# Second block: attention jobs between eighths of the projection tiles, maps combined in one operation, head outputs written over the queries

## The reference, cut to what matters

```python
for l in range(2):                       # last = (l == 1)
    h, hc = modulate(rms(x)), modulate(rms(ctx))
    u, q, k, v = split_heads(h @ w_in);  uc, qc, kc, vc = split_heads(hc @ w_in)
    q, k = rope(q), rope(k)
    # diff_attn, per head: a0, a1 = softmax of two half-heads' scores
    #   o = (a0 - lam * a1) @ v     over all 768 keys (context and latent)
    mix = concat([pool_mixer(u), rms_head(o) * g_sub * (1 - lam_init)])
    x = x + ga * (mix @ w_out);  x = x + gm * mlp(x)
    if not last: the same for ctx, with its own 256 keys
```

## Time and profile before

| | us |
|---|---|
| median of 3 runs (lowest to highest) | 3059.66 (3058.81 to 3061.07) |
| the profiled execution | 3054.51 |
| its span in the profile | 3052.7 |
| layer 0: input stage, from 1411.09 | 176.2 |
| layer 0: attention, from 1587.31 | 152.6 |
| layer 1: input stage, from 2372.36 | 137.2 |
| layer 1: attention, from 2509.59 | 117.8 |

### The profile page before, as it was taken

How to read it: one execution, slowest core, us unless ns; L and a number is a source line. 1 busy time by engine, 2 the same in 40 slices (tenths; PEclk the granted TensorE clock), 3 DMA queues, 4 the chain that set the end, 5 groups by cost and what they waited for, 6 DMA issues and landing times.

```text
span 3052.7 us, 48183 instructions
## 1 busy us (share of the span) xinstructions
PE 2763.0 (91%) x20880; PEld 2199.7 (72%) x20880; DVE 1473.0 (48%) x2538; ACT 883.8 (29%) x1436; POOL 102.1 (3%) x168
## 2 busy tenths in 40 slices
PE   3999988888899999997968799999999888899998
PEld 1767566677788788886845478888888665678886
DVE  2455556678743544444256454333333546454344
ACT  2434411110133322233214433122232314333222
POOL 0000011112100000000010000000000000000000
PEclk7999999999999999998978799999999988999999
DMA  6000456630033222222010012111211120122320
GB/s 243 28 28 29 168 192 223 221 107 3 4 124 124 78 95 87 106 83 80 28 55 1 4 52 81 58 56 56 83 56 56 39 77 7 55 83 83 111 83 28
DMA packets 17922, 242.42 MB, mean 79 GB/s; under 512 B 2016, under 2 KB 2176, under 8 KB 2864
## 3 DMA queue, kind: packets, MB, share of 16 engines
q1 hardware_dynamic: 16416, 231.94, 20.8%
q0 software_dynamic: 1296, 7.39, 0.6%
HBM read 237.23 MB, written 2.10 MB: 78 GB/s over the span
## 4 chain that ended last, share of the span: by engine, by line
PE 84%; DVE 10%; ACT 3%; issue 2%; DMA 1%; POOL 0%; DVEq 0%; ACTq 0%; POOLq 0%
PE ps L317 58%; PE ps L1205 7%; PE ps L1912 2%; PE ps L379 2%; PE ps L1763 2%; PE ps L1933 2%; PE ps L859 1%; PE ps L815 1%; DVE hh L470 1%; DMA cst<-in_consts 1%; PE ps L861 1%; PE ps L860 1%; DVE mvec L2030 1%; PE ps L390 1%; DVE sq L466 1%
## 5 line engine op out<-in xcount | busy, mean ns | idle before, releaser
L317 PE MATMUL ps<-hh,ws 128*128 128x512 f32 x3936 | 943.0, 399 | 48.7 <-DVE hh L470 26.8
L317 PEld LDWEIGHTS ps<-hh,ws 128*128 128x128 f32 x3936 | 745.8, 191 | 228.6 <-issue 61.7
L308 DVE TENSOR_TENSOR ws<-raw,ws 128x1024 fp32r<-128x1024 f32 x295 | 360.0, 1223 | 220.5 <-ACT ws L300 220.4
L300 ACT ACTIVATE ws<-raw 128x1024 fp32r<-128x1024 f32 x295 | 308.7, 1049 | 482.5 <-PE ps L317 433.1
L317 PE MATMUL ps<-g,ws 128*128 128x512 f32 x1536 | 364.4, 395 | 0.0
L317 PEld LDWEIGHTS ps<-g,ws 128*128 128x128 f32 x1536 | 286.1, 188 | 67.2
L1205 PEld LDWEIGHTS ps<-ar 64*64 64x64 f32 x6656 | 212.8, 140 | 51.0 <-issue 32.1
L1516 DVE SCALAR_TENSOR_TENSOR xT<-ps,mods,xT 128x512 f32<-128x512 f32 x120 | 90.1, 751 | 327.3 <-PE ps L317 327.3
L1205 PE MATMUL ps<-ar 64*64 64x64 f32 x6656 | 228.5, 225 | 15.2 <-issue 7.2
L317 PE MATMUL ps<-gg,ws 128*128 128x512 f32 x960 | 226.1, 395 | 0.0
L317 PEld LDWEIGHTS ps<-gg,ws 128*128 128x128 f32 x960 | 180.2, 188 | 43.7
(11 more groups left out here) (295 smaller groups left out, 2761.0 us busy)
## 6 DMA issues: line engine op xcount, KB each, us to landing
raw<-in_w_ada SPq DMA_DIRECT2D x36, 2048.0 KB, 8.6
raw<-in_w_m SPq DMA_DIRECT2D x32, 2048.0 KB, 8.4
raw<-in_w_mlp SPq DMA_DIRECT2D x16, 2048.0 KB, 8.4
raw<-in_w_in SPq DMA_DIRECT2D x8, 2048.0 KB, 8.3
raw<-in_w_mg SPq DMA_DIRECT2D x8, 1536.0 KB, 6.6
raw<-in_w_out SPq DMA_DIRECT2D x6, 2048.0 KB, 8.4
raw<-in_w SPq DMA_DIRECT2D x5, 2048.0 KB, 8.5
xT<-in_xT POOLq DMA_DIRECT2D x1, 2048.0 KB, 16.0
```

Source lines behind the costliest of these rows:

```text
L300: e.activation(w_of(n)[0], pieces[n][2], ACT.Copy).then_inc(*hi(n))
L308: e.tensor_tensor(l, pieces[n][2], h.bitcast(F32), ALU.subtract).then_inc(*lo(n))
L317: m = e.matmul(o, a, b, start=n == 0, stop=n == 3 * kt - 1)
```

## The change

The input stage keeps u's first tile, v, and the first two tiles of k and of q. The other seven tiles (k2, q2, k3, q3, u1, u2, u3), their rotations and the poolings of u1 to u3 move into the attention. The jobs now go head by head (in layer 0 a head's four latent jobs, then its two context jobs), so a head needs only its own k and q tile.

`steps2` lays out the attention as steps. In step n TensorE does the scores of job n, a third of this step's eighths, the v products of job n - 2, a third, the transposes of job n - 1, the last third, and at most one product: a rotation, a pooling or a norm. VectorE does the maxima and weights of job n with the step's other work between them, ScalarE the exponentials of job n, then the copy of the output of job n - 2 and of the transposes of job n - 1. The eighths are spread evenly over the steps, in layer 0 over steps 0 to 21, in layer 1 over steps 0 to 13.

Further: both halves' score banks are awaited first and the two halves' products alternate; scores have one pair of banks each, transposes are in banks 7 and 4, outputs in bank 4 too, tiles and single products take banks 5 and 6 in turn. The two maps are combined in one operation (second map times a ratio plus first map, unnormalised); the norm takes the missing factor in by a second product with ones of a diagonal of the squared sums. A head's outputs are copied over its queries, squared and scaled there. The 0.125 is folded into q. Pooling works in place in the held slot, cleared once. The softmax's buffers are in a second held `raw` slot, so one slot is left for weights from block b on. The parts of `mix` are split (`act_mix`, `dve_mix`) from the step after the last eighth on, and the output projection's first tile waits for each of them instead of for the end.

The weights' columns are laid out as blocks a (u0, k0, q0, k1), b (q1, k2, q2, k3), c (q3, u1, u2, u3) beside v. In a step that follows a finished tile both engines split tiles up to the third behind it.

```diff
+        def in_blocks(l, w):
+            tag = f"in{l}"
+            a = comes(f"{tag}a", w[0], 4096)
+            columns(f"{tag}a", a, [(0, (l, "u", 0))])
+            slot2[l] = hold(f"mix{l}")
             dense(f"{tag}v", w[3], pk=2, pc=512)
+            columns(f"{tag}a", a, [(1, (l, "k", 0)), (2, (l, "q", 0)), (3, (l, "k", 1))])
+            b = comes(f"{tag}b", w[1], 4096)
+            columns(f"{tag}b", b, [(0, (l, "q", 1)), (1, (l, "k", 2)), (2, (l, "q", 2)), (3, (l, "k", 3))])
+            soft2[l] = hold(f"att{l}")
+            c = comes(f"{tag}c", w[2], 4096)
+            columns(f"{tag}c", c, [(0, (l, "q", 3)), (1, (l, "u", 1)), (2, (l, "u", 2)), (3, (l, "u", 3))])
         mlp_blocks("m0", I["w_mlp1"], I["w_mlp2"])
...
+            dense(f"o{l}0", I[f"w_out2_{l}"][0])
+            let_go(f"att{l}")
             let_go(f"mix{l}")
+            dense(f"o{l}1", I[f"w_out2_{l}"][1])
             mlp_blocks(f"m{l + 1}", I[f"w_m1_{l}"], I[f"w_m2_{l}"])
...
+            jobs = [(kind, qb, t4) for t4 in range(4) for kind in range(1 if last else 2) for qb in range(2 if kind else 4)]
...
+            def steps2():
+                weight = [1 if f[2] else 2 for f in flows]
+                parts = [(f, k) for f in range(len(flows)) for k in range(KT)]
+                todo, over = KT * sum(weight), nj - 2
+                steps, given, spent = [], 0, 0
+                for n in range(nj + 1):
+                    mine = []
+                    while given < len(parts) and spent * over < todo * (n + 1):
+                        spent += weight[parts[given][0]]
+                        mine.append(parts[given])
+                        given += 1
+                    steps.append(mine)
...
+                    for f, k in mine:
+                        if k < KT - 1:
+                            continue
+                        name, m, j = flows[f]
+                        put("evict", n + 1, flows[f])
+                        if f == len(flows) - 1 or flows[f + 1][0:2] != (name, m):
+                            put("split", n + 1, tile_piece[l, name, m] + 3)
+                        if name == "u":
+                            a = max(n + 2, free[j])
+                            put("sums", a, (m, j))
+                            put("mean", a + 1, (m, j))
+                            b = product_at(a + 2, ("pool", m, j))
+                            put("out", b + 1, (m, j))
+                            free[j] = b + 1
+                            ready[m, j] = b + 2
+                        elif j == 0:
+                            b = product_at(n + 2, ("turn", name, m))
+                            put("turned", b + 1, (name, m))
+                            first_use = min(i for i, x in enumerate(jobs) if x[2] == m)
...
+                end = max(n for n, mine in enumerate(steps) if mine)
+                for i, (kind, qb, t4) in enumerate(jobs):
+                    if i + 1 == nj or jobs[i + 1][0::2] != (kind, t4):
+                        put("square", i + 3, (t4, kind))
+                        b = product_at(i + 4, ("norm", t4, kind))
+                        put("root", b + 1, (t4, kind))
+                        put("scale", b + 2, (t4, kind))
...
             def pe_scores2(e, i):
                 kind, qb, t4 = jobs[i]
                 n = cols_of(i)
                 for p in range(2):
+                    for t in ps.take((l, "s2", i, p), (2 * p,), 2):
                         e.wait_ge(*t)
+                for a in range(0, n, 512):
+                    b = min(n, a + 512)
+                    for p in range(2):
+                        q = (qc if kind else q2)[halves(p), t4, qb * 128:qb * 128 + 128]
+                        m = e.matmul(ps.two((l, "s2", i, p))[:, a:b], q, kall[halves(p), t4, a:b], start=True, stop=True)
+                        if b == n:
+                            m.then_inc(*acc((l, "s2", i, p)))
...
+            def pe_flip2(e, i, half):
+                blocks = list(range(cols_of(i) // 128))[4 * half:4 * half + 4]
+                if blocks:
+                    e.wait_ge(*dve[l, "w2", i])
+                    for t in ps.take((l, "t2", i, half), (4 if half else 7,)):
+                        e.wait_ge(*t)
...
             def pe_out2(e, i):
                 kind, qb, t4 = jobs[i]
+                nt = cols_of(i) // 128
+                for half in range(1 if kind else 2):
+                    e.wait_ge(*act[l, "t2", i, half])
+                for t in ps.take((l, "o2", i), (4,)):
+                    e.wait_ge(*t)
...
+                    dense_bank.append(11 - dense_bank[-1])
+                    for t in ps.take((l, name, m, j), (dense_bank[-1],)):
                         e.wait_ge(*t)
...
+                bank = (11 - dense_bank[-1],)
...
             def tensor_attention2(e):
+                for i in range(6):
+                    e.wait_ge(*act[l, "v", i])
+                e.wait_ge(*dve[(l, "q", 0, 0), "end"])
+                for i, parts, at in steps2():
+                    if i + 1 < nj:
+                        kind, qb, t4 = jobs[i + 1]
+                        for name in "kq":
+                            e.wait_ge(*dve[(l, name, t4, 0), "end"])
+                            if not last or name == "k":
+                                e.wait_ge(*act[l, name, t4, 1])
+                        pe_scores2(e, i + 1)
+                    third = (len(parts) + 2) // 3
+                    for f, k in parts[:third]:
+                        pe_flow_part2(e, f, k)
+                    if 0 <= i - 1 < nj:
+                        pe_out2(e, i - 1)
+                    for f, k in parts[third:2 * third]:
+                        pe_flow_part2(e, f, k)
+                    if 0 <= i < nj:
+                        pe_flip2(e, i, 0)
+                        pe_flip2(e, i, 1)
+                    for f, k in parts[2 * third:]:
+                        pe_flow_part2(e, f, k)
+                    for x in at("product"):
+                        pe_product2(e, *x)
...
+            def scalar_attention2(e):
+                e.wait_ge(*lo[final[load_before[f"att{l}"]]])
+                for i, parts, at in steps2():
+                    for name, m, j in at("evict"):
+                        if name == "u":
+                            act_up(e, m, j)
+                        else:
+                            act_keep(e, name, m, j)
+                    for x in at("root"):
+                        act_head_root2(e, *x)
+                    for n in at("split"):
+                        split_hi(e, n)
+                    for x in at("square"):
+                        act_head_square(e, *x)
+                    for p in range(2):
+                        if i + 1 < nj:
+                            act_soft2(e, i + 1, p)
+                    if 0 <= i - 1 < nj:
+                        act_out2(e, i - 1)
+                    if 0 <= i < nj:
+                        act_flipped2(e, i, 0)
+                        act_flipped2(e, i, 1)
...
+                e.reciprocal(rc, su1).then_inc(*dve())
+                e.scalar_tensor_tensor(head_sums(t4)[kind][:, qb:qb + 1], su0, 128.0 * EPS, su0, ALU.mult,
+                                       ALU.mult).then_inc(*dve((l, "sums2", i)))
+                e.wait_ge(*dve.prev())
+                e.scalar_tensor_tensor(ratio, rc, nlam, su0, ALU.mult, ALU.mult).then_inc(*dve())
+                e.wait_ge(*dve.prev())
+                e0, e1 = e_buf[i % 2][:, 0:n], e_second[:, 0:n]
+                e.scalar_tensor_tensor(e0, e1, ratio, e0, ALU.mult, ALU.add).then_inc(*dve((l, "w2", i)))
...
+            def vector_attention2(e):
+                for i, parts, at in steps2():
+                    for x in at("turned"):
+                        dve_turn_sin(e, *x)
+                    for x in at("out"):
+                        dve_pool_out(e, *x)
                     if i + 1 < nj:
+                        dve_max2(e, i + 1)
+                    for n in at("split"):
+                        split_lo(e, n)
+                    for x in at("turned"):
+                        dve_turn_cos(e, *x)
+                    for x in at("sums"):
+                        dve_pool_sums(e, *x)
+                    for x in at("mean"):
+                        dve_pool_mean(e, *x)
+                    for x in at("square"):
+                        dve_diagonal(e, *x)
+                    for x in at("scale"):
+                        dve_head_out(e, *x)
+                    if i + 1 < nj:
+                        dve_weights2(e, i + 1)
+                    for x in at("mix"):
+                        dve_mix(e, *x)
+                dve.also(f"mix{l}")
             def tensor_out2(e):
                 ps.use = range(8 - len(out_rows))
...
+                            [((l, "out", m, j), of(h), w, (l, "mixlo", j) if m == 0 else None)
+                             for j, h, hid, x, w, bufs, bank in out_rows])
```

509 lines of the change are left out of this document (268 added, 241 removed).

## The result

The changed kernel took **2959.53 us** (median of 4 runs, 2955.17 to 2965.07), the kernel before 3060.36 beside it: a ratio of 0.9667, 95% interval 0.9644 to 0.969. Forecast were 2967 and a gain of 92.9 us; the gain is 100.8.

A forecast was written before the change was run, and what follows sets the result against it. No engine was full: TensorE waited on VectorE and ScalarE in four stretches. Input stages, TensorE's work and waits summed to 263.1 us (from 328.8) and 227.8 (from 255.0), a gain of 92.9: median 2967, range 2935 to 3008.

The forecast's parts named there:

- The input stages: Before each layer's attention: first tile, v, further tiles, rotations and pooling products on TensorE, 81.2 and 80.8 us.
- TensorE's own work, at full clock: In the attentions: jobs, seven deferred tiles, rotations, pooling products and norms, 148.9 us in layer 0, 118.0 in layer 1.
- wait for block c: In each attention: ScalarE stands at the third input block's first split until its load lands; TensorE waits 9 and 11 us.
- idle in the tail: After the last tile part VectorE still has jobs, pooling and splits to finish; TensorE idles 14 and 12 us.
- small waits: In the attentions: products closing a step wait about 1 us for a tile's eviction, plus one handoff; 7 and 3 us.
- clock: In the attentions: products after a stall and in the tail run at a lowered clock, 3 us in each layer.
- the link that I had called level: Second half of the transposes waits for the last job's output copy: 5.0 us against 5.2 of TensorE work.
- VectorE's room: Layer 0's attention: VectorE busy 128 of 149 us, close but under; falling behind was named the likeliest way to be wrong.
- A: Rival on score products: the halves run one after the other, 33 us more, 3000 us; chance 0.12.
- B: Rival on the attentions: short products keep the clock at 0.78 and 0.83, 66 us more, 3033 us; chance 0.07.
- C: Rival on the waits: load half as late (10), tail half as long (13), no small waits, 2934 us; chance 0.10.
- D: Rival on the attention steps: VectorE and ScalarE take turns in one chain, 45 us slower, 3105 us; chance 0.04.

The follow-up runs named there:

- e1: The changed kernel with the first tile of weight block c split one tile later: 2936.1 us, 0.9581 of the kernel before.
- e9: e1's kernel with three extra VectorE passes over the second map in every job: 2954.2 us, 0.9654 of the kernel before.
- e2: The changed kernel with score products in the old form, each half awaiting its own banks and running by itself: 2965.0 us, 0.9674 of the kernel before.
- e4: The kernel before with only the new score form, both halves' banks awaited first and halves alternating: 3075.2 us, ratio 1.004.
- e8: e1's kernel with all deferred eighths packed into the first half of the steps: 2963.7 us, 0.9684 of the kernel before.
- e3: The changed kernel with one extra VectorE pass over the second map in every job: 2963.1 us, 0.9669 of the kernel before.
- e7: e1's kernel with the eighths spread over two steps less: 2951.8 us, 0.964 of the kernel before.
- e10: e1's kernel with the widest pooling first and layer 0's eighths spread over one step more: 2942.2 us, 0.9623 of the kernel before.
- e11: e1's kernel with the widest pooling first and layer 0's eighths spread over two steps more: 2943.1 us, 0.9624 of the kernel before.

## Why the prediction was right

**The input stages** were forecast at 81.2 and 80.8 us and took 82.3 and 81.0. Layer 0's row has 1.22 us of idle time, the wait of the first scores for a rotation, which the sum left out. Layer 1's wait of the v products for the context's norm, forecast at 5.5, is there; TensorE's timeline of the kernel after:

```profile
2319.53 3.75 PE L1778 MATMUL ps<-ws,hc 128*128 128x512 f32 x8 [5.59 <-DVE hc L486]
```

**The attentions** were forecast at 181.9 and 147.0 and took 176.4 and 143.4. Of the 7.9 us by which the change brought more than forecast, 5.5 and 3.6 come from these two, less 1.3 from the input stages. Term by term:

| term | forecast 0, 1 | measured 0, 1 |
|---|---|---|
| TensorE's own work, at full clock | 148.9, 118.0 | about 151, 119 |
| wait for block c | 9, 11 | 7.2, 9.2 |
| idle in the tail | 14, 12 | 8.9, 7.8 |
| small waits | 7, 3 | 3.2, 2.7 |
| clock | 3, 3 | about 6, 4.5 |

Idle is the length of the attention less TensorE's busy time (19.3 and 19.7 us). The last line is an estimate from the busy time and the granted clock of the stretches at under full clock (4.93 us at 0.61 is 1.9 lost, 6.30 at 0.52 is 3.0, the tail's 8.38 at 0.68 some 3), and the first is what is left.

*The third block.* The mechanism is as forecast, and e1 prices it. From the step's start in layer 0 (its scores, at 1522.83) TensorE came to the second transposes after 12.6 us instead of 14, with 5.4 of work ahead of them instead of 5. The load was issued 2.7 us after the start and not 3.3, since the rotation's part ran beside the scores, and it was there 7.6 us later instead of the 8.3 taken from the earlier trace rows. What I had too small is the price behind the gap: 3.0 us of half clock in layer 1, as much as I had charged for the whole layer.

*The tail* is the term that was mis-sized. Its length was right: 32 us forecast from job 21's scores to the output projection, and it took 32.8 (those scores start at 1641.33). VectorE was the engine of the tail, busy 24.4 of 28.2 us in this window of the kernel after:

```profile
1641.00:1669.20 28.20, 20.01 (x111) 14.04 (x111) 24.37 (x59) 17.02 (x44) 0.00 (x0) 0.88 0.00 1
```

The error was in the 18 us that I gave TensorE in it. Job 21's scores are followed by the last seven eighths, 2.8 us for which my 18 (three jobs, norms, poolings) had no room, and several of the last products ran at half clock: TensorE was occupied for 24 of the 32.8 us, so 9 were idle and not 14. The clock, charged at 3, took part of this back.

*Small waits* were half of the forecast in layer 0 and near it in layer 1. In layer 0 the longest stand where I had put them, ahead of a product that closes a step (1.23 and 0.88 us). In layer 1 the longest (1.18 us) stands ahead of a second half of the transposes. Two more of that kind, 1.25 and 1.38 us and counted with the tail, wait for the output's copy, the link that I had called level; TensorE's timeline of the kernel after:

```profile
2513.30 0.41 PE L2010 MATMUL ps<-cst,raw 128*128 128x128 f32 x2 [1.38 <-ACT ar L2137]
```

*VectorE's room.* Forecast at 128 of 149 us in layer 0, it was busy for 117.1. That was the point on which I said I would be most wrong, and e9 shows how much room was left: a third of 59.5 us more showed.

**The rivals.** A (the halves one after the other): the groups took 1.56 us, and e2 shows that the order doesn't matter; the long form of 2.61 goes when both banks are awaited first (e4), so it was a bank freed late. B (the clock keeps falling): granted 0.95 over both attentions, and 1.00 in the steps with cover. The Trainium skill (TensorE: Matmul & The Clock Gate, A second HAM failure mode: psum-queue depth-cycling) tells of a kernel whose short idles made the clock swing. These traces don't show that: from 2427 to 2515 us in layer 1 the steps cycle through all eight banks with waits of up to 1.38 us, at a granted clock of 1.00. C (the waits hide): wrong on the block, which waited at nearly full price (7.2 and 9.2 us of 9 and 11), and right by half on tail and small waits (22.6 us of the 36 forecast, where C had 13). D (the two engines take turns): out by e9. What the time was forecast from, TensorE's own work with other engines beside it, is what e8 shows directly: take the eighths away from half of the jobs and 24.5 us come back. How the whole 100.8 us divide is not shown: no run leaves out the new order of the jobs, the separate banks or the eighths altogether; e3 prices the folded maps at about 5 us.

**What failed of the expectations** behind the result: e4's first (3 us, measured 12), e7's size (6 to 8 us, measured 13), and the gain promised for e10 and e11. e1 gained slightly more than its 16 to 20 us (20.4 in the attentions), since layer 1 fell to 131.2 and not 133.

## What to carry to other kernels

Where TensorE waits in each small job for maxima and exponentials, laying slices of a dense product between the job's pieces hides the loop, and keeps the clock up; the slices should last until shortly before the last job (stopping two jobs earlier cost 13 us here). Going on to the last job brought nothing, since pooling, its product and its split still hang on the last slice. When work is interleaved by a rule ("split up to the third tile behind"), look for the step in which the rule asks for something whose load that very step releases: here one constant was worth 20 us in the two attentions. And a shorter instruction group gained by waiting for everything first is no gain if the wait moves ahead of it (e4): shorten what holds the bank, or put other work in front.
